# Diffusion-transformer layer with routed experts: the merge's second half tile by tile, three shifts added before their transposes, and the router products with their operands exchanged

## The reference

```python
def rms_norm(x, g):
    y = x * lax.rsqrt(jnp.mean(jnp.square(x), axis=-1, keepdims=True) + EPS)
    return y * g
...
def merge_branches(oa, ob, ga, gb, p):
    mix = jax.nn.sigmoid(ga) * (oa @ p['w_proj_a']) + jax.nn.sigmoid(gb) * (ob @ p['w_proj_b'])
    return mix @ p['w_out']
...
def hierarchical_moe(h, p):
    ...
    lg = (t @ p['w_router_group'] + p['b_router_group'])
    g_sel = jnp.argmax(lg, axis=-1)
    g_w = jax.nn.softmax(lg, axis=-1)[ar, g_sel][:, None]
    le = (t @ p['w_router_expert'] + p['b_router_expert'])
    le_sel = le.reshape(n_tok, N_GROUPS, EXPERTS_PER_GROUP)[ar, g_sel]
    top_v, top_i = lax.top_k(le_sel, TOP_K)
    w_pair = g_w * jax.nn.softmax(top_v, axis=-1)
    e_id = g_sel[:, None] * EXPERTS_PER_GROUP + top_i
    y = routed_experts(t, e_id, w_pair, p['w_e1'], p['w_e3'], p['w_e2'])
...
def channel_sublayer(x, sh, sc, gt, p):
    h = rms_norm(x, p['g_pre_ffn']) * (1 + sc) + sh
    return x + gt * rms_norm(hierarchical_moe(h, p), p['g_post_ffn'])
...
    x = x + g1 * rms_norm(merge_branches(oa, ob, ga, gb, p), p['g_post_mix'])
    x = channel_sublayer(x, sh2, sc2, g2, p)
```

## Time and profile before

| | us |
|---|---|
| median of 3 runs | 1235.66 |
| lowest and highest | 1233.38, 1235.70 |
| the profiled execution | 1230.81 |
| its span, first to last instruction | 1229.0 |
| PE busy in the span | 1146.0 (93%) |
| DVE busy | 840.3 (68%) |
| ACT busy | 701.0 (57%) |
| POOL busy | 311.1 (25%) |

### The profile page before, as it was taken

The page is one execution under the profiler, slowest core; times in us unless marked ns, Lnnn a source line. Parts: engine busy times, 40 slices in busy tenths (PEclk is TensorE's granted clock), DMA queues, the critical chain, the costliest instruction groups (busy, mean ns, idle before and its releaser), DMA issues. The chain is left out here.

```text
span 1229.0 us, 16928 instructions
## 1 busy us (share of the span) xinstructions
PE 1146.0 (93%) x5993; PEld 917.5 (75%) x5993; DVE 840.3 (68%) x882; ACT 701.0 (57%) x810; POOL 311.1 (25%) x304
## 2 busy tenths in 40 slices
PE   4999999999788989999499999999999999999996
PEld 2677787778676778788378888887888878888773
DVE  3643242113788754617869999988999998998986
ACT  4332233223666641235268787787787778788754
POOL 1022131000113011002204334433433433443310
PEclk9999999999899999999799999999999999999999
DMA  9634534555501116321499999999999999999964
GB/s 360 218 120 146 139 125 157 180 181 184 190 1 62 61 51 233 131 66 35 148 380 379 380 377 372 373 361 361 351 366 359 351 368 362 358 363 360 358 249 190
DMA packets 151013, 301.27 MB, mean 245 GB/s; under 512 B 12031, under 2 KB 18304, under 8 KB 150322
## 3 DMA queue, kind: packets, MB, share of 16 engines
q1 hardware_dynamic: 135792, 271.07, 61.5%
q0 software_dynamic: 15008, 29.47, 7.3%
q10 hardware_dynamic: 162, 0.05, 0.0%
HBM read 290.68 MB, written 32.67 MB: 263 GB/s over the span
## 5 line engine op out<-in xcount | busy, mean ns | idle before, releaser
L1282 PE MATMUL psum<-w_hi,act_hi 128*128 128x512 f32 (+1 forms) x1248 | 497.5, 399 | 13.7 <-DVE w_lo L2032 6.3
L1284 PE MATMUL psum<-w_hi,act_lo 128*128 128x512 f32 (+1 forms) x1248 | 484.5, 388 | 0.0
L1283 PE MATMUL psum<-w_lo,act_hi 128*128 128x512 f32 (+1 forms) x1248 | 483.8, 388 | 0.0
L1282 PEld LDWEIGHTS psum<-w_hi,act_hi 128*128 128x128 f32 x1248 | 235.8, 189 | 80.7 <-DVE w_lo L2032 15.8
L1284 PEld LDWEIGHTS psum<-w_hi,act_lo 128*128 128x128 f32 x1248 | 235.5, 189 | 49.5
L1283 PEld LDWEIGHTS psum<-w_lo,act_hi 128*128 128x128 f32 x1248 | 236.2, 189 | 43.5
L2032 DVE TENSOR_TENSOR w_lo<-raw_extra,w_hi 128x2048 fp32r<-128x2048 f32 x96 | 217.2, 2289 | 45.3 <-ACT w_hi L1148 45.3
L2032 DVE TENSOR_TENSOR w_lo<-raw_mix,w_hi 128x2048 fp32r<-128x2048 f32 x96 | 219.2, 2288 | 12.3 <-ACT w_hi L1148 12.3
L1148 ACT ACTIVATE w_hi<-raw_mix 128x2048 fp32r<-128x2048 f32 x96 | 184.0, 1916 | 35.7 <-PE psum L1284 27.0
L1148 ACT ACTIVATE w_hi<-raw_extra 128x2048 fp32r<-128x2048 f32 x96 | 180.6, 1913 | 6.2 <-PE psum L1284 6.2
L1741 DVE TENSOR_TENSOR w_lo<-raw_mix,w_hi 128x2048 fp32r<-128x2048 f32 (+1 forms) x24 | 52.8, 2201 | 145.2 <-ACT w_hi L943 145.1
(11 more groups left out here) (305 smaller groups left out, 1272.6 us busy)
## 6 DMA issues: line engine op xcount, KB each, us to landing
raw_mix<-in_w_e SPq DMA_DIRECT2D x96, 1024.0 KB, 8.0
raw_extra<-in_w_e SPq DMA_DIRECT2D x96, 1024.0 KB, 8.0
raw_mix<-in_w_in SPq DMA_DIRECT2D x16, 1024.0 KB, 5.5
raw_mix<-in_w_ada SPq DMA_DIRECT2D x16, 1024.0 KB, 7.0
ada_first<-in_w_ada SPq DMA_DIRECT2D x8, 1024.0 KB, 14.3
gates_scratch<-rows POOLq DMA_DIRECT2D x20, 256.0 KB, 3.2
y_scratch<-lam SPq DMA_DIRECT2D x1, 5120.0 KB, 16.9
yrow<-gates_scratch POOLq DMA_DIRECT2D x20, 256.0 KB, 4.4
```

What stands on the lines that cost most here:

```text
L1282: pe.matmul(out, a_hi(ka_), w_hi[:, kw, :], start=s, stop=False)
L1283: pe.matmul(out, a_hi(ka_), w_lo[:, kw, :], start=False, stop=False)
L1284: ins = pe.matmul(out, a_lo(ka_), w_hi[:, kw, :], start=False, stop=e)
```

## The change

The products of units 24 and 25 run tile by tile: both units for tile 0, then both for tile 1, and so on, so that unit 25 is wanted one product after unit 24. ACT therefore makes unit 25's high half after the second tile of the first half, and DVE's split of the first expert's unit moves behind the gating. DVE's order in the second half is one tile after another, with one `shifted_h` a tile: for tiles 0 to 2 (`SHIFTED = 3`) the shift is added before the transpose, and `transpose_h2` waits for it. The router product exchanges its operands: it loads the 128 columns of `h2T_v` and streams the 36 of `wr`, which gives 128 x 36 directly in its place in bank 7. `logits`, `logit_rows`, `shl` and `rlT` are gone. The shift product does the same: DVE spreads the sample's shift over 128 columns (`shift_b`), TensorE multiplies, and DVE adds the result to the bias once (`br_late`); tiles 3 and 4 get `br_late`, tiles 0 to 2 `br`, in two adds.

```diff
@@ TensorE
-            for n in range(2):
+            def merged(n, u, i):
+                s = 22 + 2 * n + u
...
+            for u in range(2):
+                pe.wait_ge(lo_done, 22 + u + 1)
...
+                if u == 0:
+                    pe.wait_ge(shift_wide, 1)
+                    for k in range(KD):
+                        ins = pe.matmul(bank(7)[:, LOGIT_SHIFT:LOGIT_SHIFT + NR], shift_b[:, k * P:(k + 1) * P], wr_v[:, k, :], start=(k == 0), stop=(k == KD - 1))
+                    ins.then_inc(rt_mm, 1)
+
+            for i in range(NT):
+                pe.wait_ge(y_cp, i + 1)
                 for u in range(2):
...
+                    pe.wait_ge(lo_done, 24 + u + 1)
+                    merged(1, u, i)
 
             def transpose_h2(i):
-                pe.wait_ge(h2_part, i + 1)
+                pe.wait_ge(h2_done if i < SHIFTED else h2_part, i + 1)
...
-                    ins = pe.matmul(bank(2 + i % 2)[0:NR, 0:P], wr_v[:, k, :], h2T_v[i % 2][:, k * P:(k + 1) * P], start=(k == 0), stop=(k == KD - 1))
+                    ins = pe.matmul(bank(7)[:, i * NR:(i + 1) * NR], h2T_v[i % 2][:, k * P:(k + 1) * P], wr_v[:, k, :], start=(k == 0), stop=(k == KD - 1))
@@ ScalarE
             for i in range(NT):
                 merged_rows(0, i)
-            split_hi(25)
+                if i == 1:
+                    split_hi(25)
             early(0, [0])
...
             for i in range(NT):
                 merged_rows(1, i)
-                if 0 < i < NT - 1:
-                    x1_squares(i - 1)
+                if i < NT - 1:
+                    x1_squares(i)
...
             h2_columns(0)
-            x1_squares(NT - 2)
             h2_columns(1)
-            logit_rows(0)
+            x1_squares(NT - 1)
             h2_columns(2)
...
@@ VectorE
+            ve.tensor_copy(shift_b[:, :].rearrange("p (k n) -> p k n", k=KD), shift[:, 24:24 + KD, 1].unsqueeze(2).broadcast_to([P, KD, P])).then_inc(shift_wide, 1)
...
-            merged_mean_square(0)
             for i in range(NT):
+                merged_mean_square(i)
                 gated(1, i)
-                if i:
-                    mean_square(i - 1)
                 new_x(i)
-                if i + 1 < NT:
-                    merged_mean_square(i + 1)
                 if i:
                     scaled_h(i - 1)
...
+                mean_square(i)
+                if 0 < i <= SHIFTED:
+                    shifted_h(i - 1)
+                if i == 1:
+                    ve.wait_ge(rt_mm, 1)
+                    ve.tensor_tensor(br_late[:, :], bank(7)[:, LOGIT_SHIFT:LOGIT_SHIFT + NR], br[:, :], ALU.add).then_inc(shift_wide, 1)
```

More of the change, by code:

```diff
@@ L195, in build @@
         h2T_v = [h2T[:, :], pt[:, 0:D]]
[L196 removed]
+        shift_b = pt[:, D:2 * D]
+        br_late = orow[:, 0:NR]
         mtmp = osq[:, :]
@@ L549, in build @@
         SUM_BANK = [0, 2, 5, 0, 2]
+        SHIFTED = 3
+        LOGIT_SHIFT = 256
         def h2_bank(i, j):
@@ L853, in x1_root @@
                 po.tensor_tensor(stat[:, 40 + i:41 + i], stat[:, 32 + i:33 + i], half[:, 0:1], ALU.pow).then_inc(x1rs, 1)
-            merged_root(0)
-            for i in range(1, NT):
+            for i in range(NT):
                 merged_root(i)
-                x1_root(i - 1)
-            x1_root(NT - 1)
+                x1_root(i)
             po.wait_ge(h2_done, NT)
@@ L1552, in _ @@
             transpose_mix(NT - 1)
-            for n in range(2):
-                for u in range(2):
[L1556 to L1571, removed]
+            def merged(n, u, i):
+                s = 22 + 2 * n + u
+                sl = slice(i * P, (i + 1) * P)
+                product(bank(i), [(4 * u + kk, kk) for kk in range(4)], whi(s % HL), wlo(s % HL),
+                        lambda k: ah[:, k, sl], lambda k: al[:, k, sl], u == 0, u == 1).then_inc(tile_mm, 1)
@@ new lines, in _ @@
+            for u in range(2):
+                pe.wait_ge(lo_done, 22 + u + 1)
+                for i in range(NT):
+                    if u == 0:
+                        pe.wait_ge(mh_done, 2 * i + 2)
+                        pe.wait_ge(ml_done, 2 * i + 2)
+                    merged(0, u, i)
+                if u == 0:
+                    pe.wait_ge(shift_wide, 1)
+                    for k in range(KD):
+                        ins = pe.matmul(bank(7)[:, LOGIT_SHIFT:LOGIT_SHIFT + NR], shift_b[:, k * P:(k + 1) * P], wr_v[:, k, :], start=(k == 0), stop=(k == KD - 1))
+                    ins.then_inc(rt_mm, 1)
@@ L1602, in _ @@
             router(1)
-            logits(0)
+            transpose_h2(3)
             router(2)
-            logits(1)
-            transpose_h2(3)
-            logits(2)
+            router(3)
             transpose_h2(4)
-            router(3)
             router(4)
-            logits(3)
-            logits(4)
             pe.wait_ge(m_ready, 1)
@@ L2027, in _ @@
             mix_low(NT - 1)
+            shift = modc[:, :].rearrange("p (j s) -> p j s", s=2)
+            ve.tensor_copy(shift_b[:, :].rearrange("p (k n) -> p k n", k=KD), shift[:, 24:24 + KD, 1].unsqueeze(2).broadcast_to([P, KD, P])).then_inc(shift_wide, 1)
             split_lo(24)
@@ L2084, in _ @@
             ve.tensor_copy(h2T_v[(NT - 1) % 2][:, 512:1024], bank(h2_bank(NT - 1, 1))).then_inc(h2t_v, 1)
-            for i in range(2, NT):
-                shifted_h(i)
-            ve.wait_ge(rl_done, NT)
+            shifted_h(NT - 1)
+            ve.wait_ge(rt_mm, 1 + NT)
+            ve.wait_ge(shift_wide, 2)
             L = rL[:, :].rearrange("p (t n) -> p t n", t=NT)
-            link(ve.tensor_tensor(L, bank(7)[:, 0:NT * NR].rearrange("p (t n) -> p t n", t=NT), br[:, :].unsqueeze(1).broadcast_to([P, NT, NR]), ALU.add))
+            for a, b_, row in ((0, SHIFTED, br), (SHIFTED, NT, br_late)):
+                ins = ve.tensor_tensor(L[:, a:b_, :], bank(7)[:, a * NR:b_ * NR].rearrange("p (t n) -> p t n", t=b_ - a),
+                                       row[:, :].unsqueeze(1).broadcast_to([P, b_ - a, NR]), ALU.add)
+            link(ins)
             def s5(x):
```

39 lines of the change are left out of this document (11 added, 28 removed).

## The result

The changed kernel takes 1241.01 us (median of 7 runs, 1232.78 to 1245.18) against 1233.38 for the kernel before on the same chip (7 runs, 1230.29 to 1235.70): a ratio of 1.0063, 95% interval 1.0037 to 1.0088. It is slower by 0.6%, where "the same" was forecast with 0.75.

The account below looks back on a forecast made before the run. TensorE was taken to bound the kernel, its chain ending the changed stretch. Terms summed to +0.28 us at the bias add, +0.4 with the second add: 1236.0 us on the median 1235.66; range 1233.0 to 1237.8, with clock cases 1231.8 to 1238.6.

Parts of the forecast that it names:

- What bounds the stretch: Second half of merge and router up to the logits: TensorE's own chain ends it; everything after follows the bias add.
- What the swap does to a product: Router products: with 128 columns loaded the load limits each pass, so a product still costs 1.78 us, 0.111 a pass.
- The rival by which the swap pays: Router and shift products: passes follow the streamed columns, a product takes 0.65 us, time -5.3 us; chance 0.06.
- Term 1: Shift product in the merge: loading 128 columns instead of 36 takes it from 0.86 to 2.00 us, +1.14 us.
- Term 2: Merge's second half, tile by tile: same 120 matmuls, unit 25's halves ready with 5.3 us in hand, 0.
- Term 3: Elementwise work in the merge's second half: tile 2's squares no longer hold back tile 4's ACT copy, -0.53 us.
- Term 4: Start of the first router product: 581.24 us against 580.63, +0.61 us from the shift product's cost and the freed copy.
- Terms 5 and 6: First router product to bias add: logit transposes gone -0.55, uncovered copies before last product +0.86, earlier add -0.65, second add +0.08 us.
- The rival on the clock: Experts' start: full clock returns later, as long again as 8.2 us, total +4.5 us; chance 0.09.

Follow-up runs that it names:

- the trace without the fall: Changed kernel (36 streamed columns) with the fifth tile's transposes ahead of the fourth router product; its fastest execution, traced, 1229.35 us; median 1236.92 us, ratio 1.0039.
- the better version: Changed kernel with 108 streamed columns, fifth tile's transposes ahead of fourth router product, all five shifts added early, no shift product: 1229.08 us, ratio 0.9976.
- the run of 80 passes: Kernel before plus 40 useless fp32 products behind the shift product in mid-merge, 128 columns loaded, 36 streamed: 1246.78 us, ratio 1.0112.

## Why the prediction was wrong

**What bounds the stretch: right.** TensorE's chain sets the end in each trace; the add's 9.15 us came back as 9.17 at the experts' first transposes.

**What the swap does to a product: right at full clock.** "0.111, bounds 0.10 and 0.12 us": R0 of after has (583.57 - 581.76)/16 = 0.113 us a pass, and R2 in the trace without the fall (587.38 - 585.67)/16 = 0.107. The load sets it nearly alone: with 108 columns R3 of the better version takes 1.77 us (592.65 to 594.42), 0.06 more than R2 with 36. The rival by which the swap pays, at 0.65 us a product, is dead. (The row of `L1516` that the prediction reads stops at its window's end; whole it is 16 passes in 1.95 us, and gives the same (1.95 - 0.275)/15 = 0.112.)

**Term 1**, +1.14: measured +0.93; the product costs 1.79 us, 16 passes without the 0.22 for the turn-over. **Term 2**, 0: no wait. **Term 3**, -0.53: T0 to R0 went from 3.05 us (577.58 to 580.63) to 2.54, -0.51, also in the kernel without the swap. **Term 4**, R0 at 581.24: it came at 581.76, or 581.09 without the 0.67 us by which this execution was late ahead of the shift product.

**Terms 5 and 6: the steps that failed**, in their unsaid condition, "1.87 a router product, 1.02 a transpose group", as if TensorE kept full clock. With 108 columns it does, and then they hold: R0 to the add 12.90 us (586.10 to 599.00) where 13.31 were laid out (581.24 to 594.55); T4 to R4 1.91 for 1.88; R4 to the add 2.04 for 2.00. The 0.4 us of difference is a transpose group of 0.87 instead of 1.02 (587.98 to 588.85) where a product with 128 loaded columns follows, three times. The whole came out at ratio 0.9993 and 1.0003 (108 and 72 columns), which is the forecast "+0.4 us" within what can be measured. With 36 columns the clock fell, and the same steps took 21.66 us from R0 to the add (581.76 to 603.42): 8.76 us more than with 108.

**The rival on the clock had the wrong place.** It let the clock hurt only at the experts' start, and priced a late return at up to +4.5 us. The return varies by itself, 2.8 to 5.6 us behind the first expert product; the 8.8 us came from a fall that set in right behind the first router product. I had asked what streaming fewer columns does to a pass, not what it does to the clock. The trace of before has no long run of passes with 128 loaded and few streamed columns: at most 16 of `L1516` (64 streamed) and 8 of `L1318` (2 streamed). The shift product alone, 16 such passes between long matmuls, didn't make it fall either (the window 536.0 to 538.3 us has 1.00).

The Trainium skill's page "TensorE: Matmul & The Clock Gate", section "Why this matters for your kernels", has the clock kept by leaving no long idle gaps between bursts. The trace doesn't agree for this stretch: TensorE was busy in every one of the windows in which the clock fell, behind a wait of 0.63 us ahead of R0 in the router and behind none in the run of 80 passes. It agrees at the experts' start, where filling the idle time brought the clock back.

**The range and the signs.** The range's upper end, 1238.6, doesn't hold the prediction's own late return: +4.5 on 1235.66 is 1240.2. The base was high too: three runs gave 1235.66, the later sets of before 1233.38, 1232.55, 1231.51 and 1232.72. Of its signs the shift product (1.87 us for 1.95) and the wait ahead of R4 (0.88 for 0.8) came as named; the add missed 594.3 by 9.1 us, and full clock returned outside 619 to 623 us, the sign of being wrong that came true, as a result of the fall ahead of it.

**What stays open.** Why the clock falls in these runs with 36 streamed columns and not with 72; and why one execution in some keeps it. The changed kernel's runs at 1232.78 to 1233.94 us, with mean clock 0.975 where the others have 0.962 to 0.972, are probably those, but no trace of them was taken. The 72 columns have one trace behind them and 12 executions. The separate worth of the early shifts of tiles 0 to 2 was not measured by itself.

## What to carry to other kernels

When a change gives TensorE's passes fewer streamed and more loaded columns, the load sets the pass, and a run of such fp32 passes can cost the clock even with TensorE always busy: read the granted clock over the run, in more than one trace, and if it falls, stream more columns, even useless ones, which here cost under 0.1 us a product at 72 and 108. Choose the order of the operands for what it removes behind the product (small transposes, copies), not for the streamed columns. Where a serial chain leaves TensorE idle ahead of a long TensorE-bound stage, useless products in its waits can bring the clock back early, here for some 3 us.

## What the runs showed of the hardware

- TensorE's clock fell to 1.2 GHz with TensorE busy without a gap, behind the first router product with 128 loaded and 36 streamed columns in five traces of six, and between 539 and 540 us in the run of 80 such passes that began at 537.36; with 72 (one trace), 108 (five) or 128 (one) streamed columns it stayed at 2.4 GHz. Once down it stayed so through all the other passes of that kind (to 552.7 us), and came back between 556 and 557 us, among matmuls of 512 columns.
- At half clock a pass with 128 loaded columns and 36 streamed takes 0.204 us ((588.53 - 585.26)/16). At full clock the first router product takes 0.113, 0.115 and 0.118 us a pass with 36, 72 and 108 streamed columns, the second 0.107, 0.109 and 0.111: nearly the same.
- The return of full clock at the experts' start comes 2.8 to 5.6 us behind their first product, from trace to trace of one kernel too.
- Executions of one kernel, the one before too, differ by 6 us and more (30 of before on one chip: 1229.83 to 1239.67). In the traces of the changed versions part of that is a shorter dip of the clock in the attention, long before the change: the window 400 to 420 us has 1.00 in some traces and 0.79 to 0.91 in others, with T0 some 4 to 5 us later.
